# First block's remaining projections ahead of the halo, new buffer layout, row scaling shared with GpSimd, queries without a trip through memory

## The reference, cut to what matters

```python
h = rms_norm(x, g_pre_mix)
proj = h @ w_in                         # q, k, v (768 each), u (256), gates (2048)
q, k = apply_rope(q), apply_rope(k)     # 12 heads of 64
for gi, (window, dilation) in enumerate(((128, 1), (512, 4), (2048, 16))):
    o_g, lse_g = dilated_window_attention(q[gi], k[gi], v[gi], window, dilation)   # 4 heads each
wts = softmax(stack(lses), axis=0)      # over the three head groups
o_attn = sum(wts * outs)
y_pool = multiscale_pool(u, w_pool_mix, pool_scale)
merged = sigmoid(gate_a) * (o_attn @ w_proj_attn) + sigmoid(gate_p) * (y_pool @ w_proj_pool)
x = x + rms_norm(merged @ w_out, g_post_mix)
a, b = split(rms_norm(x, g_pre_ffn) @ w_gate_up)
x = x + rms_norm((silu(a) * b) @ w_down, g_post_ffn)
```

## Time and profile before

| | us |
|---|---|
| median of 3 runs (range) | 974.02 (973.38 to 975.49) |
| the profiled execution's own time | 975.52 |
| its span on the slowest core (core 4) | 972.5 |
| the eight cores' spans | 964.8 to 972.5 |
| busy in the span: TensorE, VectorE, GpSimd, ScalarE | 937.4, 473.3, 353.9, 342.1 |

### The profile page before, as it was taken

One profiled execution on the slowest core, in us unless ns is written; L12 is line 12 of the kernel. 1 busy time (PEld: TensorE's weight loads), 2 busy tenths in 40 slices (PEclk: granted clock), 3 DMA queues, 4 the chain that ended last, 5 costly groups with the idle time before them and its releaser, 6 DMA issues.

```text
span 972.5 us, 15020 instructions; the slowest of 8 cores (964.8 to 972.5 us)
## 1 busy us (share of the span) xinstructions
PE 937.4 (96%) x5416; PEld 472.7 (49%) x5416; DVE 473.3 (49%) x560; ACT 342.1 (35%) x555; POOL 353.9 (36%) x334
## 2 busy tenths in 40 slices
PE   8879999989999999999999999999999999999997
PEld 3446776644554454444444444444444444444443
DVE  4889886686887867575454111111223111111323
ACT  4667426553445446434483111110101111110211
POOL 1447855467865584775693101110001000000000
PEclk8899999998999999999999999999999999999999
DMA  8936852451223477554377666563233545350221
GB/s 203 277 120 224 184 112 75 96 149 44 45 66 80 74 151 148 168 133 116 109 240 186 116 125 114 106 111 85 89 130 109 84 68 86 66 87 1 87 109 65
DMA packets 41224, 112.76 MB, mean 116 GB/s; under 512 B 5984, under 2 KB 14688, under 8 KB 41056
## 3 DMA queue, kind: packets, MB, share of 16 engines
q0 software_dynamic: 14432, 45.65, 27.7%
q1 hardware_dynamic: 26320, 66.07, 20.7%
q10 hardware_dynamic: 400, 0.08, 0.0%
HBM read 136.14 MB, written 21.30 MB: 162 GB/s over the span
## 4 chain that ended last, share of the span: by engine, by line
PE 84%; issue 4%; DVE 4%; DMA 3%; POOL 2%; ACT 2%; DVEq 0%; ACTq 0%; POOLq 0%; SPq 0%
PE ps L524 74%; PE ps L522 10%; DMA wq<-wq 1%; DMA wgs<-wg 1%; POOL x1b L522 1%; POOL st L522 1%; DVE junk L522 1%; ACT xsb L522 1%; DVE PT L522 1%; DMA tab<-tab 1%; DVE x1b L522 1%; DVE rt L522 0%; ACT junkd L522 0%; ACT xs L522 0%; DVE val L522 0%
## 5 line engine op out<-in xcount | busy, mean ns | idle before, releaser
L524 PE MATMUL ps<-hT,wgu 128*128 128x512 bf16 x1232 | 294.6, 379 | 0.0
L524 PEld LDWEIGHTS ps<-hT,wgu 128*128 128x128 bf16 x1232 | 120.4, 98 | 144.9
L522 DVE TENSOR_TENSOR ffT<-ps,sa 128x512 bf16<-128x512 f32 x88 | 60.8, 691 | 230.5 <-PE ps L522 226.4
L522 ACT ACTIVATE sa<-ps 128x512 f32<-128x512 f32 x88 | 52.4, 596 | 239.9 <-PE ps L522 239.9
L524 PE MATMUL ps<-wdna,ffT 128*128 128x512 bf16 x512 | 115.7, 379 | 1.0 <-issue 0.5
L522 POOL DMA_DIRECT2D wgu<-wgu x44 | 23.6, 537 | 245.8 <-PE ps L522 226.1
L524 PE MATMUL ps<-hT,wgs 128*128 128x512 bf16 x448 | 108.6, 383 | 3.1 <-ACT tg L522 2.1
L522 POOL TENSOR_TENSOR k<-rt 128x512 bf16<-128x512 f32 (+1 forms) x36 | 80.0, 2229 | 42.7 <-DVE rt L522 42.7
L522 DVE TENSOR_TENSOR rt<-ps,tab 128x512 f32<-128x512 f32 (+1 forms) x120 | 76.1, 669 | 20.2 <-PE ps L522 14.7
L522 ACT ACTIVATE junkd<-ps 128x1024 bf16<-128x1024 f32 (+1 forms) x33 | 32.8, 993 | 147.0 <-PE ps L522 147.0
L524 PEld LDWEIGHTS ps<-wdna,ffT 128*128 128x128 bf16 x512 | 50.0, 98 | 61.8 <-issue 1.9
(11 more groups left out here) (149 smaller groups left out, 1308.3 us busy)
## 6 DMA issues: line engine op xcount, KB each, us to landing
wgu<-wgu POOLq DMA_DIRECT2D x44, 512.0 KB, 6.2
xst<-xo SPq DMA_DIRECT2D x16, 512.0 KB, 8.3
xsth<-xh SPq DMA_DIRECT2D x16, 512.0 KB, 6.1
wgs<-wg POOLq DMA_DIRECT2D x16, 512.0 KB, 6.0
xin<-xo SPq DMA_DIRECT2D x16, 512.0 KB, 5.9
x1s<-x1b SPq DMA_DIRECT2D x16, 512.0 KB, 4.4
xin<-x1s SPq DMA_DIRECT2D x16, 512.0 KB, 4.3
out<-x1b SPq DMA_DIRECT2D x15, 512.0 KB, 2.9
```

The lines of the kernel that those rows point to most:

```text
L522: e.ops.append(lambda q, m=method, a=a, k=k, s=sem.sem, v=step: getattr(q, m)(*a, **k).then_inc(s, v))
L524: e.ops.append(lambda q, m=method, a=a, k=k: getattr(q, m)(*a, **k))
```

## The change

1. `f1(0)`, the second stage of the first own block, is issued right behind that block's third-group queries and keys, with its weights loaded between row tiles 7 and 8 (`LOADS`), no longer after the halo's rows. `att_g2` now has `f1(1)` behind it, `att(s)` has `f1(s+2)`.
2. The buffers are laid anew so that this can be: `v01`, `k0`, `k1`, `q01` no longer share space with the halo's row buffers; those lie in the masks' and in unused parts of `k2`/`v2`'s region.
3. The gain moves out of the weights into the PSUM eviction of each transposed tile (`to_feature_major`); `gained` and the product on the gate weights in `merge` are gone.
4. Square sums: of odd tiles 1 to 7 by `bn_stats`/`bn_aggr` on VectorE, of all others on ScalarE. Odd tiles from 9 on (12 of them) are scaled by GpSimd.
5. `by_head` is gone: all scores are two matmuls over 32 rows, with heads laid as in the third group.
6. The third group's scores may use two PSUM pairs (`sc2g`), and its results are copied to `acc` by VectorE, no longer by ScalarE. The four cosine tables made on TensorE load their terms one by one.

```diff
--- before.py
+++ after.py
+POOL_FROM = 8
...
-WV_AT = 10
+LOADS = ["x3", "q2", "t", "k2", "x4", "t", "k0", "k1", "q0", "q1", "v0", "v1", "x4", "t", "x4", "t", "v2"]
...
-PART = {"norm": -615, "norm_h": -320, "qk2": 0, "k2h": -175, "v2": 650, "v2h": 15, "f-1": 90, "f0": 40, "f1": 0, "f2": 40, "f3": 0, "g2": -435,
...
+PART = {"norm": -1680, "norm_h": -505, "qk2": 5, "k2h": -400, "v2": -100, "v2h": -490, "f-1": -150, "f0": 30, "f1": -10, "f2": 80, "f3": 65,
...
+    sc2, sc2g, ov2 = pairs([0], True), pairs([0, 4]), pairs([2], True)
...
+    k2 = P.sb("k2", [128, 2, 2, 16, 128], BF16, R2 + 8 * KB)
+    v2 = P.sb("v2", [128, 2, 16, 6, 64], BF16, R2 + 24 * KB)
...
+    xsth = P.ring("xsth", [128, D], F32, [R_MASK, R2 + 28 * KB, R2 + 32 * KB, R2 + 24 * KB, R3 + 16 * KB])
+    terms = P.ring("terms", [96, 2, 512], BF16, [R2 + 24 * KB, R2 + 26 * KB])
+    xsb = P.ring("xsb", [128, D], BF16, [R3 + 12 * KB, R3 + 14 * KB], False)
+    junk = P.ring("junk", [128, D], BF16, [R_VAL], False)
     wq2 = P.sb("wq2", [128, 2, 8, 128], BF16, R3 + 16 * KB)
-    wk2 = P.sb("wk2", [128, 2, 8, 128], BF16, R3 + 20 * KB)
-    wv2 = P.sb("wv2", [128, 8, 256], BF16, R3 + 24 * KB)
-    xsb = P.ring("xsb", [128, D], BF16, [R3 + 28 * KB + i * 2 * KB for i in range(2)], False)
-    junk = P.ring("junk", [128, D], BF16, [R3 + 32 * KB + i * 2 * KB for i in range(2)], False)
-
-    terms = P.sb("terms", [96, 4, 2, 512], BF16, R4)
+    wk2 = P.sb("wk2", [128, 2, 8, 128], BF16, R6)
+    wv2 = P.sb("wv2", [128, 8, 256], BF16, R4 + 24 * KB)
...
+    v01 = P.sb("v01", [128, 21, 6, 64], BF16, R3)
...
+    K01 = [R3 + 20 * KB, R3 + 24 * KB, R3 + 16 * KB]
...
+    q01 = P.ring("q01", [128, 2, 2, 512], BF16, [R3 + 28 * KB, R3 + 32 * KB])
...
+    def w_load(dst, src, name, after=()):
+        d = pool.dma(dst, src, dsem(name), after=behind() + list(after))
+        loads.append(d)
+        return d
...
+    for what in LOADS:
+        if what[0] == "x":
...
+            for c in (2 * int(what[1]), 2 * int(what[1]) + 1):
+                d_w01["q%d" % c] = w_load(wq01[:, c, :, :], wq_d[c], "d_w01_q%d" % c)
...
-    def gained(w, d, n):
-
-        return dve.tensor_tensor(out=w, in0=w, in1=gpre.unsqueeze(2).to_broadcast([128, 8, n]), op=ALU.mult, after=[d, v_gains])
...
+    def to_feature_major(src, rs, ring, xb, gain, dst, after, war, col=1, by_pool=False):
+
+        if by_pool:
+            cp = pool.tensor_scalar(out=xb[:, :], in0=src, scalar1=rs[:, col:col + 1], scalar2=1.0, op0=ALU.mult, op1=ALU.mult, after=[rs.tok] + after)
+        else:
+            cp = act.activation(out=xb[:, :], in_=src, func=AF.Copy, scale=rs[:, col:col + 1], after=[rs.tok] + after)
...
-        if gain is None:
-            h = dve.tensor_copy(out=dst, in_=psb, after=[tr] + war)
-        else:
-            h = dve.tensor_tensor(out=dst, in0=psb, in1=gain.unsqueeze(2).to_broadcast([128, 8, 128]), op=ALU.mult, after=[tr, v_gains] + war)
+        h = dve.tensor_tensor(out=dst, in0=psb, in1=gain.unsqueeze(2).to_broadcast([128, 8, 128]), op=ALU.mult, after=[tr, v_gains] + war)
...
-                if e == 1:
-                    sqs.append(dve.scalar_tensor_tensor(out=j_[:, :], in0=src, scalar=1.0, in1=src, op0=ALU.mult, op1=ALU.mult, accum_out=sums[:, e:e + 1], after=[u.tok]))
...
-        g_w01[name] = gained(d, d_w01[name], 256 if name[0] == "v" else 128)
...
-    def by_head(tile, n, after):
-
-        i = n_heads[0]
-        n_heads[0] += 1
-        down = sp.dmas([(qk_d[i, h, :, :, 0:n].rearrange("half f n -> f half n"), tile[32 * h:32 * h + 32, :, :]) for h in range(4)], dsem("d_qo%d" % i), after)
-        return [sp.dmas([(tile, qk_d[i, :, :, :, 0:n].rearrange("(pair hh) half f n -> (hh half f) pair n", hh=2))], dsem("d_qi%d" % i), [down])]
...
-                Q[s].tok[g] = by_head(Q[s][:, g, :, :], 512, done)
+                Q[s].tok[g] = done
...
+    def norm_tile(i):
+        halo = i >= NT
+        P.bias = PART["norm_h" if halo else "norm"]
+        if i % 2 == 0:
+            pair[:] = [xt.pop(0), xt.pop(0)]
+            sums, sqs = st4.new(), []
+            for e, u in enumerate(pair):
+                if e == 1 and i < POOL_FROM:
+
+                    bn = bns.new()
+                    b6 = [dve.bn_stats(out=bn[:, 6 * h:6 * h + 6], in_=u[:, 512 * h:512 * h + 512], after=[u.tok]) for h in range(2)]
+                    ag = dve.bn_aggr(out=bn[:, 12:14], in_=bn[:, 0:12], after=b6)
+                    sqs.append(dve.scalar_tensor_tensor(out=sums[:, e:e + 1], in0=bn[:, 12:13], scalar=bn[:, 12:13], in1=bn[:, 13:14], op0=ALU.mult, op1=ALU.add, after=[ag]))
+                    bn.free(sqs[e])
+                else:
+                    j_ = junk.new()
+                    sqs.append(act.activation(out=j_[:, :], in_=u[:, :], func=AF.Square, scale=1.0 / 32.0, accum_out=sums[:, e:e + 1], after=[u.tok]))
...
+        cp, tr, h_ok[i] = to_feature_major(t[:, :], sums, any1, xsb.new(), gpre, (hTh if halo else hT)[:, :, j:j + 128], [],
+                                           x_cp[:NT] if halo else [], col=2 + i % 2, by_pool=i % 2 == 1 and i >= POOL_FROM)
...
+    for i in range(NT):
+        norm_tile(i)
+        if i % 4 == 3:
+            s = i // 4
+            P.bias = PART["qk2"]
+            qk2_unit("q", s, False)
+            qk2_unit("k", s, False)
+            if s == 0:
+                P.bias = PART["f0"]
+                f1(0, any1, any2)
...
-    def att_qk(pair, items, mask, after, halves=1):
-        pt, sb = PT.new(), sc2.new()
+    def att_qk(pair, items, mask, after, ring=sc2):
+        pt, sb = PT.new(), ring.new()
...
-                for half in range(halves):
+                for half in range(2):
...
-                    c = act.activation(out=acc[:, :, h, :].rearrange("p s (rho m a) -> p m rho s a", rho=4, m=4)[:, r4],
-                                       in_=ob[:, hh, :].rearrange("p (r s a) -> p r s a", r=4, s=4), func=AF.Copy, after=pvs + hTh_mm)
+                    c = dve.tensor_copy(out=acc[:, :, h, :].rearrange("p s (rho m a) -> p m rho s a", rho=4, m=4)[:, r4],
+                                       in_=ob[:, hh, :].rearrange("p (r s a) -> p r s a", r=4, s=4), after=pvs + hTh_mm)
...
-            return lambda _, h: t[PR(h), h // 2, c:c + 128]
+            return lambda half, h: t[HR(h), half, c:c + 128]
...
-            P.bias += PART["wg"]
-            wt.tok = dve.tensor_tensor(out=wt[:, :, :, :], in0=wt[:, :, :, :], in1=fap(gpre, [(0, 2), (1, 8), (0, 128)]), op=ALU.mult, after=[d, v_gains])
-            P.bias -= PART["wg"]
+            wt.tok = d
...
-    f1(0, fill1, fill2)
+    P.bias = PART["f1"]
+    f1(1, fill1, fill2)
...
-        if s < 3:
-            P.bias = PART["f%d" % (s + 1)]
-            f1(s + 1, fill1, fill2)
+        if s < 2:
+            P.bias = PART["f%d" % (s + 2)]
+            f1(s + 2, fill1, fill2)```

TensorE in the first stage of the kernel before, behind the first own block's third-group keys (`wk2`); `warmw` is constant data, `ident` transposes a tile.

```order
29 L524 MATMUL ps<-hT_31_73,wk2_55_97 128x512 x7
30 L522 MATMUL ps<-hT_31_73,wk2_55_97 128x512
31 L524 MATMUL ps<-warmw_8_50 128x512 x8
32 L522 MATMUL ps<-warmw_8_50 128x512
33 L524 MATMUL ps<-ident_1_43,xsb0_57_99 128x128 x7
34 L522 MATMUL ps<-ident_1_43,xsb0_57_99 128x128
35 L524 MATMUL ps<-ident_1_43,xsb1_58_100 128x128 x7
```

More of the change, by code:

```diff
@@ L371, in fill @@
         units = ring.units[vt.slot]
-        vt.pre = [m for x in units for m in x.old]
+        vt.pre = [m for x in units for m in x.old + x.over]
         n.start = start
@@ new lines, in build_program @@
+    P.bias = PART["w01"]
+    over_x = x_cp[NT:]
+    d_masks = sp.dma(masks[:, :, :], masks_d[:, :, :], dsem("d_masks"), after=over_x)
+    d_mix = []
+    for g in range(4):
+        c, hf = g // 2, g % 2
+        d_mix.append(pool.dma(wmixb[64 * hf:64 * hf + 64, c, 64 * hf:64 * hf + 64], wmix_d[g, :, :], dsem("d_mix%d" % g), after=[loads[-1], m_mix]))
+    P.bias = PART["v2h"]
+    m_v2.append(dve.memset(v2[:, 0, :, 1:5:3, :], 2.0, after=over_x))
+    for r in range(16):
+        v2_unit(r, True)
```

287 lines of the change are left out of this document (130 added, 157 removed).

## The result

The changed kernel takes 979.4 us (median of 5 runs), the kernel before 974.0 on the same chip: a ratio of 1.0054, 95% interval 1.0039 to 1.0068, or 5.4 us more. The forecast was 964.3 with a range of 952 to 975; the result lies above it, and the kernel became slower where it was to become faster. The profiled execution took 979.38 (span 977.5 on core 5; the eight cores 969.3 to 977.5).

What follows compares the result with a forecast made beforehand. The prediction took TensorE, 84% of the last-ending chain, as the bound. Terms +7.0 - 10.1 + 1.4 - 8.0 = -9.7 us took the profiled 975.5 to 965.8, with the median 1.5 lower at 964.3; range 952 to 975.

Steps and rivals of the forecast that it cites:

- What follows the merges is untouched.: Stages behind the merges, from the output projection on: claimed unchanged, given no term in the sum.
- The front, -10.1.: Up to the first third-group score: it comes 4.2 us later with 14.3 us more work done, so -10.1 us.
- The landing of the last own tile: Front, row loads: the last own tile lands at about 67 us, behind the ten second-stage weight loads.
- the way from landing to eviction: Front, last own tile: squares, scaling, transposes and eviction add 6.4 us, so it is done at 73 us.
- my next term: Front, TensorE behind the last own tile: 70 us of work plus 4 us of waits, first third-group score at 147 us.
- Scores, +7.0.: First two head groups: 32 score groups over 32 rows, each 0.22 us longer on TensorE, +7.0 us.
- Third group's attention, +1.4.: Third-group scores to first block's attention: 4.0 us lost in place of 2.6, +1.4 us, bounds 1 and 9 lost.
- First blocks, -8.: First blocks' attention: without gate-weight gains on VectorE, TensorE's waits, constant matmuls and low clock go, -8 us; bounds 0 and 13.
- No constant matmuls stand between 150 and 500 us: TensorE, 150 to 500 us: the absence of matmuls on constant data was named as a sign of being right.
- GpSimd's scaling.: Front, scaling of row tiles on GpSimd: 2.35 us each taken, bounds 1.2 and 4.4; above 3.25 not hidden.
- the rival that needed it, 953 us: GpSimd never in the way, all attention waits gone: scaling near 1.2 us, 953.3 us in all, chance 0.15.
- The slower one: Front, GpSimd becomes the bound: at 4.4 us a scaling, +3.7 in place of -10.1, 978.1 us, chance 0.12.

Runs made afterwards that it cites:

- e2: The changed kernel, same order, with the first four loads of rows for the output projection held until `wout` has landed; 971.7 us, ratio 0.9978 to the kernel before.
- e8: The kernel before, same order, with the 16 gains of the gate weights cut to one column each; 969.5 us, ratio 0.9952.
- e20: e2 with the loads of rows counted among themselves alone, apart from weight loads, and the changed kernel's own table; 969.5 us, ratio 0.9953.
- e15: e2 with the ten second-stage weight loads cut to a quarter of their bytes, row loads counted among themselves, table refitted; 960.4 us, ratio 0.9867.
- e4: The kernel before, same order and relay, with the first two head groups' 32 score groups run as 16 matmuls over 32 rows; 975.7 us, ratio 1.0021.
- e19: e2 with only the table of numbers that sets the order fitted anew; 964.7 us, ratio 0.9901 to the kernel before.
- e10: e2, same order, with the ten second-stage weight loads cut to a quarter of their bytes; 970.6 us, ratio 0.9970 to the kernel before.

## Why the prediction was wrong

- **"What follows the merges is untouched."** This sentence failed, and it cost most: +7.7 us (e2). An attention that ends sooner frees `xin`'s buffers sooner, and the loads that this starts collide with `wout`. I asked what the gains and the scores cost and did not ask which transfer the attention's end releases. In the changed kernel it ends 17 us sooner; the gains alone bring 2.9 of this (e8).
- **The front, -10.1.** Measured -2.9. The first half of the reasoning was right: `f1(0)` runs where constant data ran, and by the count above, as a mean over six cores, TensorE loses 1.1 us from 38 to 60 in place of 11.0. From 60 to the first score it then loses 12.3 in place of 5.4, where I had taken 4 of waits in place of 2.5. The landing of the last own tile came out at 67.3, as forecast. The sum behind it failed: the way from landing to eviction took 13.5 us and not 6.4 (waits behind other tiles in ScalarE's queue, for GpSimd and for TensorE, where I had added up durations), so the tile was evicted at 80.8 and not 73. But mending this term doesn't mend the forecast. The path from this tile does not set the mark by itself: in e20 the tile is evicted at 64.05, and the mark stays. That my next term came out, 70 us of work and 4 of waits from there (73.4 measured), was luck; in e20 it is 88.7. What does move the mark is bytes, pacing and order together (e15, 6.7 us); which of them would do with the whole weights stays open. That the loads on GpSimd's queue cost nothing was not separated by any run.
- **Scores, +7.0.** The groups cost what the earlier trace rows say, and the work by count grew by 7.1. But the sum took them as time, and on the kernel before they cost 2.0 (e4): in that stage TensorE waits for others, and with more work it waits less.
- **Third group's attention, +1.4.** +3.0, inside its bounds; in e19 this stage loses 3.4 us and not 6.9.
- **First blocks, -8.** In e2, without the collision, this stage loses 16.0 us where before lost 24.1: -8.1, as forecast. The gains alone give 4.5 of it in the old order (e8); the rest goes with the scores, whose work fills waits. So two terms were mis-sized, +2.0 and not +7.0, -4.5 and not -8.0, and their sum, -1.0 forecast and -2.5 by these runs, came out near by luck. No constant matmuls stand between 150 and 500 us, as forecast.
- **GpSimd's scaling.** 1.12 us, below my bound of 1.2 and far from the 2.35 taken. The Trainium skill (GPSIMD Engine Reference, "Engine selection") has one input roughly at VectorE's rate. The trace does not settle it: VectorE's two one-input steps over 1,024 float32 elements took 0.69 us (`gpost`) and 1.15 us (`gfin`), so GpSimd lies between the same rate and 1.6 times as long. It changed nothing, and the rival that needed it, 953 us, did not come.
- **The rivals.** The slower one needed GpSimd as the bound. Nothing in the list stood for a transfer that starts too early, nor for an order that fits badly; the chance of 0.11 for slower was small for a change that replans everything.

## What to carry to other kernels

When a stage is to end sooner, list the transfers that its end releases and what else is in flight at that time. A step that is moved forward must be followed in every in-order queue that it enters: copies that wait for TensorE, put into ScalarE's queue, held a row tile back for 13.6 us (e10). Before a sum is built on one input's arrival, ask what else stands near it: here that input came 17 us sooner and the mark did not move (e20). And when an order is planned from a table, refit it for both versions before the change is judged; here that gave 7.0 us on one side and 1.8 on the other, each from a single search.
